# Router stage of a two-layer diffusion step on one core: transposes put first into four banks, bf16 split moved from GpSimd to ScalarE and VectorE, ranks computed within the shared product

## The reference, cut to what matters

```python
scores = jax.nn.sigmoid(x @ w_router)                       # 256 x 64
sel = scores + router_bias
# two best of each of 8 groups -> 4 best groups -> 6 best experts
wsel = scores[chosen] / sum(scores[chosen]) * ROUTED_SCALE
hid = silu(x @ w_gate[e]) * (x @ w_up[e])                   # per expert, 256 wide
routed = sum over e of (hid * combine[:, e]) @ w_down[e]
shared = (silu(x @ ws_gate) * (x @ ws_up)) @ ws_down
```

## Time and profile before

| | us |
|---|---|
| median of 3 runs | 1568.79 |
| lowest and highest | 1568.09, 1568.93 |
| profiled execution, its own time | 1569.29 |
| span in its trace | 1567.5 |
| TensorE busy | 1501.9 |
| VectorE busy | 466.5 |
| ScalarE busy | 441.7 |
| GpSimd busy | 21.3 |

### The profile page before, as it was taken

How to read it: one execution, slowest core, us unless ns; L and a number is a source line. 1 busy time by engine, 2 the same in 40 slices (tenths; PEclk the granted TensorE clock), 3 DMA queues, 4 the chain that set the end, 5 groups by cost and what they waited for, 6 DMA issues and landing times.

```text
span 1567.5 us, 30939 instructions
## 1 busy us (share of the span) xinstructions
PE 1501.9 (96%) x13231; PEld 1069.8 (68%) x13231; DVE 466.5 (30%) x937; ACT 441.7 (28%) x1095; POOL 21.3 (1%) x33
## 2 busy tenths in 40 slices
PE   5999999899999999999998998899999999999996
PEld 3868768576767676767666858767676767666664
DVE  2243451612222222222223134522222222222224
ACT  2123232322222222222322022412323232323233
POOL 0000000200000000000000000200000000000000
PEclk9999999899999999999998999899999999999998
DMA  9997876459999999999995413639999999999970
GB/s 354 399 350 280 323 304 250 188 220 399 393 407 392 404 396 406 384 411 388 409 394 137 161 42 153 235 121 372 410 393 404 398 397 400 394 404 407 390 328 28
DMA packets 101443, 510.55 MB, mean 326 GB/s; under 512 B 11256, under 2 KB 19600, under 8 KB 52240
## 3 DMA queue, kind: packets, MB, share of 16 engines
q1 hardware_dynamic: 97440, 506.57, 81.8%
q10 hardware_dynamic: 3952, 3.24, 0.6%
HBM read 506.65 MB, written 3.15 MB: 325 GB/s over the span
## 4 chain that ended last, share of the span: by engine, by line
PE 92%; DVE 3%; ACT 2%; DMA 1%; SPq 1%; issue 0%; DVEq 0%; ACTq 0%
PE psum L1246 90%; PE psum L1560 1%; DMA arena<-in_hgrn_w_in 1%; SPq L375 1%; ACT arena L525 1%; DVE arena L815 0%; ACT arena L548 0%; PE psum L1707 0%; DVE arena L817 0%; DVE arena L1142 0%; DVE arena L1138 0%; DVE arena L1079 0%; ACT L536 0%; DVE arena L1071 0%; DVE arena L1075 0%
## 5 line engine op out<-in xcount | busy, mean ns | idle before, releaser
L1246 PE MATMUL psum<-arena 128*64 128x256 f32 (+9 forms) x12948 | 1465.9, 336 | 44.6 <-ACT arena L548 12.6
L1246 PEld LDWEIGHTS psum<-arena 128*64 128x64 f32 (+4 forms) x12948 | 1036.5, 136 | 469.5 <-issue 248.5
L525 ACT ACTIVATE arena<-psum 128x512 bf16<-128x512 f32 (+5 forms) x554 | 199.9, 388 | 419.3 <-PE psum L1246 320.9
L1138 DVE TENSOR_TENSOR arena<-psum,arena 128x512 f32<-128x512 f32 x128 | 88.0, 688 | 315.8 <-ACT arena L525 315.8
L525 ACT ACTIVATE arena<-arena 128x512 bf16<-128x512 f32 (+1 forms) x144 | 87.5, 617 | 111.5 <-DVE arena L1138 108.9
L1142 DVE TENSOR_TENSOR arena<-arena 128x512 bf16<-128x512 f32 x128 | 88.7, 693 | 98.0 <-ACT arena L525 98.0
L689 ACT ACTIVATE arena<-psum 128x256 f32<-128x256 f32 x64 | 24.6, 385 | 299.1 <-PE psum L1246 299.1
L1131 DVE SCALAR_TENSOR_TENSOR arena<-arena,psum 128x256 f32<-128x256 f32 x64 | 30.7, 480 | 262.0 <-ACT arena L689 262.0
L1121 DVE COPY arena<-psum 128x192 f32<-128x192 f32 x128 | 39.8, 353 | 95.9 <-PE psum L1246 95.9
L860 DVE SCALAR_TENSOR_TENSOR arena<-psum,arena 128x128 f32<-128x128 f32 x64 | 17.8, 344 | 62.8 <-PE psum L1246 62.8
L532 ACT ACTIVATE arena<-arena 128x512 f32<-128x512 f32 x20 | 12.3, 629 | 73.0 <-DVE arena L860 72.1
(11 more groups left out here) (140 smaller groups left out, 304.3 us busy)
## 6 DMA issues: line engine op xcount, KB each, us to landing
arena<-in_moe_w_gate SPq DMA_DIRECT2D x64, 2048.0 KB, 9.6
arena<-in_moe_w_up SPq DMA_DIRECT2D x64, 2048.0 KB, 14.2
arena<-in_moe_w_down SPq DMA_DIRECT2D x64, 2048.0 KB, 10.9
arena<-in_ada_w SPq DMA_DIRECT2D x24, 2048.0 KB, 14.5
arena<-in_hgrn_w_in SPq DMA_DIRECT2D x10, 2048.0 KB, 13.0
arena<-in_na_w_qkv SPq DMA_DIRECT2D x6, 2048.0 KB, 19.2
arena<-in_hgrn_w_out SPq DMA_DIRECT2D x1, 4096.0 KB, 14.0
arena<-in_na_w_o SPq DMA_DIRECT2D x1, 4096.0 KB, 12.8
```

Source lines behind the costliest of these rows:

```text
L525: return act.activation(out, in_, ACT.Copy, **kw)
L1138: dve.tensor_tensor(y_rest[:, at], psum[:, 6 + half, :], y[:, j, 0, at], ALU.subtract)\
L1246: return pe.matmul(out, lhsT, rhs, start=start, stop=stop, skip_group_check=True, **kw)
```

## The change

TensorE: the 16 transposes no longer follow the logits but go chunk by chunk with them, into banks 0 to 3, four to a bank, so that none waits for a bank to be read; the first four chunks' logits are formed between them, the last four chunks' behind all transposes. `shared(0)` no longer waits for a copy, and two of the eight products of `shared(1)` go ahead of the ranks. ScalarE: it copies each bank once, to bfloat16, ahead of the sigmoid; a sigmoid of one element stands before the copies. VectorE: it does the subtractions, the first from the bank, ahead of the selection, the second behind the selection; the order of its later steps is changed. GpSimd: no subtractions.

```diff
+        def piece(n):
+            return n % 2, slice(4 * (n // 2), 4 * (n // 2) + 4)
...
 # GpSimd
-                for part, before_it, after_it in ((0, M.htok, M.h_rest), (1, M.h_mid, M.h_low)):
-                    for n in range(4):
...
-                        pool.tensor_tensor(out, h_rest[:, a, ks], h_tok[:, part, a, ks], ALU.subtract)\
-                            .then_inc(after_it, 1)
                 pool.wait_ge(M.h_low, 4)
 # ScalarE
+                act.activation(lb_t[:, 0:1], eps, ACT.Sigmoid)
+                for n in range(4):
+                    act.wait_ge(M.htok_ps, n + 1)
+                    a, ks = piece(n)
+                    copy(h_tok[:, 0, a, ks], psum[:, n, :].rearrange("p (k t) -> p k t", t=P)).then_inc(M.htok, 1)
                 act.wait_ge(M.logits, 1)
...
-                    copy(h_rest[:, a, ks], rows)
-                    copy(h_tok[:, 0, a, ks], rows).then_inc(M.htok, 1)
 # VectorE
+                for n in range(4):
+                    a, ks = piece(n)
+                    dve.wait_ge(M.htok, n + 1)
+                    dve.tensor_tensor(h_rest[:, a, ks], psum[:, n, :].rearrange("p (k t) -> p k t", t=P),
+                                      h_tok[:, 0, a, ks], ALU.subtract).then_inc(M.h_rest, 1)
                 dve.wait_ge(M.scores, 1)
...
+                for n in range(4):
+                    a, ks = piece(n)
+                    dve.wait_ge(M.h_rest, n + 1)
+                    dve.wait_ge(M.h_mid, n + 1)
+                    dve.tensor_tensor(h_tok[:, 2, a, ks], h_rest[:, a, ks], h_tok[:, 1, a, ks], ALU.subtract)\
+                       .then_inc(M.h_low, 1)
...
+                shared_hidden(0)
                 dve.wait_ge(M.rank_ps, 1)
...
+                one_hots(M, 0, 0, 0)
...
+                shared_hidden(1)
 # TensorE
+                def turn(k):
+                    h_chunk(2 * m + 1, k)
+                    for a in range(2):
+                        ins = pe.transpose(psum[:, 2 * (k // 4) + a, (k % 4) * P:(k % 4 + 1) * P],
+                                           hT[:, k, a * T:(a + 1) * T], ident)
+                        if k in (3, 7):
+                            ins.then_inc(M.htok_ps, 1)
...
+                for k in BY_ARRIVAL[:4]:
+                    turn(k)
+                    route_chunk(k)
+                for k in BY_ARRIVAL[4:]:
+                    turn(k)
+                for k in BY_ARRIVAL[4:]:
+                    ins = route_chunk(k)
                 ins.then_inc(M.logits, 1)
-                    if n >= 2:
-                        pe.wait_ge(M.htok, n - 1)
...
-                    pe.wait_ge(M.htok, 3 + a)
...
                 pe.wait_ge(M.sh_in, 48)
-                shared(0)
+                shared(0, range(K))
+                shared(1, range(2))
...
-                shared(1)
+                shared(1, range(2, K))
```

More of the change, by code:

```diff
@@ L657, in experts_front @@
                 for n in range(4):
-                    act.wait_ge(M.htok_ps, n + 1)
-                    a, ks = n // 2, slice(4 * (n % 2), 4 * (n % 2) + 4)
-                    rows = psum[:, 6 + n % 2, :].rearrange("p (k t) -> p k t", t=P)
-                    copy(h_rest[:, a, ks], rows)
-                    copy(h_tok[:, 0, a, ks], rows).then_inc(M.htok, 1)
-                for n in range(4):
-                    a, ks = n // 2, slice(4 * (n % 2), 4 * (n % 2) + 4)
+                    a, ks = piece(n)
                     act.wait_ge(M.h_rest, n + 1)
@@ L1091, in experts_front, with shared_hidden @@
                 done()
+                for n in range(4):
+                    a, ks = piece(n)
+                    dve.wait_ge(M.h_rest, n + 1)
+                    dve.wait_ge(M.h_mid, n + 1)
+                    dve.tensor_tensor(h_tok[:, 2, a, ks], h_rest[:, a, ks], h_tok[:, 1, a, ks], ALU.subtract)\
+                       .then_inc(M.h_low, 1)
+                def shared_hidden(a):
+                    dve.wait_ge(M.sh_silu, a + 1)
+                    dve.tensor_tensor(sh_hid[:, a], sh_silu[:, a], psum[:, 6 + a, F:2 * F], ALU.mult)\
+                       .then_inc(M.hid if a else M.sh_hid, 1)
+                shared_hidden(0)
                 dve.wait_ge(M.rank_ps, 1)
@@ L1448, in experts_front @@
                 M = moe[m]
[L1449 to L1452, removed]
-                        ins = mm(psum[:, 5, a * E:(a + 1) * E], hT[:, k, a * T:(a + 1) * T], router_w[:, m, k],
-                                 k == BY_ARRIVAL[0], k == BY_ARRIVAL[-1])
-                ins.then_inc(M.logits, 1)
-                for n in range(4):
-                    if n >= 2:
-                        pe.wait_ge(M.htok, n - 1)
[L1459 to L1462, removed]
@@ L1464, in shared @@
-                def shared(a):
-                    pe.wait_ge(M.htok, 3 + a)
-                    for k in range(K):
+                def turn(k):
[5 more added lines that the diff above has]
+                            ins.then_inc(M.htok_ps, 1)
@@ new lines, in route_chunk @@
+                def route_chunk(k):
+                    for a in range(2):
+                        ins = mm(psum[:, 5, a * E:(a + 1) * E], hT[:, k, a * T:(a + 1) * T], router_w[:, m, k],
+                                 k == BY_ARRIVAL[0] and a == 0, k == BY_ARRIVAL[-1])
+                    return ins
+                for k in BY_ARRIVAL[:4]:
[5 more added lines that the diff above has]
+                    ins = route_chunk(k)
@@ L1468, in shared @@
+                ins.then_inc(M.logits, 1)
+                def shared(a, ks):
+                    for k in ks:
                         ins = mm(psum[:, 6 + a, :], hT[:, k, a * T:(a + 1) * T], ws_gu[:, k], k == 0, k == K - 1)
-                    ins.then_inc(M.sh_ps, 1)
+                    if k == K - 1:
+                        ins.then_inc(M.sh_ps, 1)
                 pe.wait_ge(M.sh_in, 48)
-                shared(0)
+                shared(0, range(K))
+                shared(1, range(2))
```

7 lines of the change are left out of this document (1 added, 6 removed).

## The result

| | before | changed |
|---|---|---|
| median, us | 1568.86 | 1557.84 |
| lowest to highest | 1568.09 to 1569.10 | 1557.31 to 1557.89 |
| span of the profiled execution | 1567.5 | 1555.5 |

The changed kernel is faster by 11.0 us; the ratio is 0.993, with an interval of 0.9915 to 0.9945. 1565.0 had been forecast, within 1563.4 to 1567.6: the direction was right, the gain nearly three times as large as forecast.

The account below looks back on a forecast made before the run. TensorE, busy 1501.9 of 1567.5 us, was taken as the bound. Per stage 1.4 + 0.8 - 0.3 = 1.9 us, 3.8 for two, took 1569.29 to 1565.5, or 1565.0 as the median; range 1563.4 to 1567.6.

Parts of the forecast that it names:

- The wait for `mask`: Router stage: TensorE's wait for VectorE's selection would vanish once GpSimd's subtractions were gone, saving 0.8 us per stage.
- VectorE's new work: Router stage: VectorE's 2.8 + 2.8 us of added subtractions would be hidden, costing nothing.
- TensorE's front: TensorE up to the first wide product: logits and transposes without waits take 10.7 us, saving 1.4 us per stage.
- The clock term: Router stage: wide products start earlier, at half clock; taken as 0.3 us lost per stage, between 0 and 0.7.
- the prediction's own sign: If right, the first gather comes 26.7 to 27.4 us after TensorE's start in the stage, 28.9 before.
- the clock comes back inside the front: Rival: full clock returns among transposes and logits, 2.6 us won per stage, 1560 in all; chance 0.04.
- Later: Rival: the clock stays down throughout `shared(0)`, 5.9 us lost against 2.2 won per stage, 1576 us; chance 0.10.
- The chain stays long: Rival: GpSimd isn't what stretches VectorE's selection; TensorE waits 3.3 us for `mask`, 1571 us; chance 0.04.
- the gain is given back in the loop: Rival: expert-loop transfers, at 0.99 of their engines, cancel the gain, 1568.8 us; chance 0.04.
- The rule that I weighed: Skill's rule: TensorE at 1.2 GHz after idleness, 2.4 GHz after being kept busy; judged not to fit small products.

Follow-up runs that it names:

- e4: The kernel before with only GpSimd's eight subtractions moved to VectorE, behind the selection; 1566.10 us.
- e3: The changed kernel with the split given back: ScalarE copies each bank twice, GpSimd does all eight subtractions, VectorE none; 1570.04 us.
- e1: The changed kernel with all 16 logit products first and all 16 transposes behind them; 1562.98 us.
- e2: The changed kernel with all 16 transposes first and all 16 logit products behind them; 1558.93 us, from 1555.81 to 1562.21.
- e6: The changed kernel with all eight products of `shared(1)` behind the ranks again; 1556.99 us.
- e7: The kernel before with four useless 512-column products in TensorE's idleness ahead of the first normed chunk; 1567.81 us.
- e9: The kernel of e4 with four useless products ahead of the router stage; 1563.67 us.
- e5: The changed kernel with four useless 512-column products in TensorE's idleness ahead of the first normed chunk; 1550.80 us.
- e8: The changed kernel with useless products ahead of both router stages, layer 1's first projection, the last transposes and each loop's last combination; 1551.30 us.
- e10: The changed kernel with two useless products ahead of the first chunk, where e5 has four; 1552.42 us.

## Why the prediction was wrong

**The wait for `mask`** was right: 0.8 us per stage gone, by the cause named. L1067 takes 0.16 us, the selection from L1056 to the end of L1082 6.0 us (291.69 to 297.70; 12.5 before, 6.0 forecast), and e4, with the streams of TensorE and ScalarE as before, shows that GpSimd's run made the difference; e3 agrees.
**VectorE's new work** was hidden, as forecast: the first four subtractions end at 291.78, 0.7 us behind the sigmoid and not ahead of it, since the logits came sooner than forecast, and hold the selection up by about 0.5 us; TensorE still had no wait. The second four end at 301.5, and the ranks are read at 301.79, about 1 us after they were there; that stays beneath the wide products, and the gather's loads (305.52) follow without a wait.

**TensorE's front** was forecast to save 1.4 us per stage and saved 3.8 (12.14 to 8.3). At least 1.8 of that is clock: 16 logit records behind 288.75 at 0.116 us in place of 0.226. Another 0.6 is spacing at half clock, 1.17 us a group where I had worked out 1.33 from records that had stood alone. The remaining 1.4 is what had been forecast. So the first gather came 23.0 us after the start (305.52), where the prediction's own sign was 26.7 to 27.4.

**The clock term** is the step that failed. I had it at -0.3 us per stage, between two bounds that both assumed a return under the wide products, and gave a return inside the front a chance of 0.04. It gave +2.8: the 1.8 above, and 1.0 since the wide products of `shared(0)` all ran at full clock (6.9 us, from 290.8 to 297.7, against 7.9). The argument against had been that the clock had not risen "in nine microseconds of almost unbroken logits and transposes". The runs show that these nine microseconds were two different things: 7.5 us of logit products alone, during which the clock rose in none of the seven stages that have them at half clock (before, e1, e4, e2's layer 0), and then transposes; in every stage where it rose ahead of the wide products, it did so during transposes or within 1.3 us behind them. Unbroken transposes behind the logits had it back after 9.8 us (e1), transposes among the logits after 5.6 to 7.3 (changed, e3, e6). So I had counted the new front as 1.4 us of removed waits, when what it did to the clock, 2.8 us, was worth twice that. Whether the waits between the transposes had kept the clock down before isn't shown: in e7 and e9 it came back during transposes with such waits in them (0.32 us), in e2's layer 0 it didn't during all 16. Why a mixture does it sooner stays open.

The rivals: *the clock comes back inside the front* is what happened, 1560 worked out and 1557.8 measured. *Later* did not occur in the changed kernel, but e4's layer 1 (16.5 us) and e2's layer 0 (12.8) show that it can. *The chain stays long* is ruled out by the changed kernel's own 6.0 us and by e4, *the gain is given back in the loop* by the sum: 2 x 6 us in the stages, 12.0 in the span.

The rule that I weighed had foretold the right side here, but the runs bear out only half of its reason: the Trainium skill, "TensorE: Matmul & The Clock Gate", section "The two states you'll see", ties the clock to how busy TensorE was. In both stages of every trace without fillers the clock fell around the end of the 4.1 us of idleness, and fillers in that idleness kept it up (e5). But in e7 TensorE was busy at 1.00, as the profile counts it, when the clock fell. The same page, section "Part 4: PE-mode transpose", says that the full clock doesn't engage for transposes; in e2's layer 1 nothing else had run since the fall, and the clock came back.

What remains open: whether 64-column products without any stall let a clock fall that is up; how the same instructions gave 12.8 and 3.6 us within one execution of e2, and what separated e8's fastest execution from its others. Also not tried: the mixture with GpSimd's run but without its `mask` wait.

## What to carry to other kernels

When an edit removes short waits or changes the order of small products behind an idle stretch of TensorE, don't price only the waits: look at the granted clock for the whole stage, and at which kinds of products stood between its fall and its return. Where TensorE idles for microseconds ahead of light work, useless wide products in the gap are worth a try: two or four of them gained another 5 to 7 us here, and in the traces the clock stayed up. And small VectorE instructions that last as long as GpSimd's beside them are a chain to free, but here that alone gained 2.8 us (e4), the new order alone nothing (e3), and both together 11.0. Last, read both stages and more than one execution: one trace can show either outcome of e2.

## What the runs showed of the hardware

In none of the seven stages with some 7 us of float32 products of 64 columns at half clock did the clock rise during them, with TensorE busy 1.00 (before, e1, e4, e2's layer 0). Behind wide products it fell among such products, 2.3 to 3.7 us after the first (e7, e9, four stages), with short stalls in front that may have a part in it. Float32 transposes of 128 columns, with nothing else since the fall, had it back at 1.00 in e2's layer 1, and did not in its layer 0.

TensorE's waits and the clock behind them: after 3.2 and 3.3 us (e3) it had fallen by the end of the wait; after 1.6 us (e7) it fell 1.2 and 0.9 us later, behind five products of 64 columns; after 0.8 us it did not fall; and after 2.42 us ahead of the mixture (e10, both stages of one execution) it did not fall either.
